# Moving one more slice of a modulation product from VectorE to TensorE, in a prologue that streams its weights from memory

## The chip, the cores and the metric

The kernel runs on one core of one Trainium2 chip. The metric is device time in microseconds, from the start of the program to its end. The engines carry these names: PE is TensorE (matmuls; PEld is its weight loads), DVE is VectorE, ACT is ScalarE, POOL is GpSimd and SP is SyncE, which here only starts transfers. An engine works through its own instructions in order, and engines wait for each other with semaphores that count up.

## What is computed

Two transformer-like blocks in float32, 256 tokens of width 2048. Only the start of the first block matters here. A condition vector c is multiplied with a large matrix, and the result shifts and scales a normed input, which then meets the weights `a_w_in`:

```python
silu_c = jax.nn.silu(c)                              # c: 1 x 2048
m_l = (silu_c @ ada_w[i] + ada_b[i]).reshape(bsz, 1, N_MOD, D_MODEL)   # ada_w: 2048 x 12288
n_l = modulate(rmsnorm(h_lat, norm_g[i, 0]), m_l[:, :, 0], m_l[:, :, 1])   # h * (1 + scale) + shift
z = jax.nn.gelu(h @ w_in)                            # in chunk_mlp_mix, with h = n_l; w_in: 2048 x 8192
```

The shift is the first 2048 columns of the product and the scale the second 2048. Everything else in the first block follows on z, and the second block on the first.

## The kernel before, in words

**The prologue.** Shift and scale are made in four groups g = 0 to 3 of 512 output columns each, and with each group four more tiles of 128 input channels of n_l (k = 4g to 4g+3) become ready. For a group, eight slices d = 0 to 7 of `ada_w` are loaded into `mods`, which has four slots: slice t = 8g + d goes to slot t % 4. A slice is 256 rows of the matrix times 512 columns of the shift and 512 of the scale, and two transfers bring it (L368). SP starts them in order, and before slice t it waits until slice t - 4 has been used.

**Two ways to use a slice.** On DVE (`mod_group`) a slice takes two operations on 128x1024 elements (L1086 for the first of a group, L1089 for the others), which add slice times condition value into `acc`. On PE (`mod_column`, L1790) a slice takes 16 small matmuls, with 128x128 of the slice as the weights and one column of the condition as the moving operand, so that the sum over rows comes out in a few PSUM columns. `PE_MOD` lists the slices of each group that go to PE: 6 in group 0, and 2 in groups 1, 2 and 3. The rest goes to DVE. When DVE has added its last slice, `mod_last` (L1801) sums `acc` over the partitions with eight matmuls of the same small kind. `mod_gain` on DVE (L1098 to L1101) adds the partial sums and writes `acol`, which is the group's gain, and `mcol`, which holds its shift.

**The weight units.** `a_w_in` comes in slabs of 1 MB into `raw` (L348), four slabs deep, and each slab is two units of 128x2x512. For each unit ACT writes a rounded copy `whi` (`cast`, L521), DVE writes the remainder `wlo` (`lo`, L1029), and PE does 12 matmuls of 512 columns (`tok_unit`, L1722). Group g has the six units u = 6g to 6g+5. With a group's gain, ACT and DVE make the four tiles of n_l: DVE writes `n1full` (L1137) for the first two and ACT for the others, ACT writes the rounded `xth` (L627), and DVE writes the remainder `xtl` (L1141). The group's first unit needs the first two `xtl` tiles and the `lo` of unit 6g, and its second unit needs the other two.

**The order on each engine,** for group g:

- PE: `mod_last(g)`, units 6g to 6g+3, `mod_column(g+1, 2)`, units 6g+4 and 6g+5. Group 0 has `mod_column(0, 6)` ahead of all.
- DVE: the adds of the group (with `lo` of the previous group's last two units after slices 0 and 1), `lo` of units 6g and 6g+1, `mod_gain(g)`, `n1full`, `xtl`, `lo` of units 6g+2 and 6g+3.
- ACT: the casts of units 6g and 6g+1, then, with the gain there, the tiles, then the other casts.
- SP: the slices 0 to 7 of the group (each behind its slot), three slabs, and then the next group. Behind group 3 it sends 20 more slabs and 16 transfers for another part of `ada_w`. A slab waits until `lo` of the units that lay in its place is done.

Slice 6 of groups 1 to 3 lies in the slot of slice 2, and so it waits for `mod_column(g, 2)` on PE. Behind the prologue follow the rest of the first block and the whole second block, both with PE at work almost throughout.

Of the kernel before, what the change touches and what calls it, by code (L numbers as in the profile page):

```python
# [24 lines left out]
P = 128  # L25
# [41 lines left out]
QUAD_AT = tuple(12 + 3 * n for n in range(16))  # L67
Q_TURN_AT = (10, 20, 29, 38)
TURN_BANK = (2, 3, 4)
PE_MOD = ((6,), (2,), (2,), (2,))  # L70


def first_unit(u):
# [7 lines left out]
    return sum(2 for i in range(4) for e in range(8) if e not in PE_MOD[i] and (i, e) <= (g, d))  # L81


def mod_columns(g, last=True):

    return 2 * g + 3 + last


HALVES = list(range(16, 32)) + list(range(16))
# [94 lines left out]
def program(nc, a, out):  # L184
    with ExitStack() as ctx:
# [156 lines left out]
        def _(sp):  # L342
# [14 lines left out]
            for g in range(4):  # L357
                for d in range(8):
                    t = 8 * g + d
                    if t >= 4:  # L360
                        g0, d0 = (t - 4) // 8, (t - 4) % 8
                        if d0 in PE_MOD[g0]:
                            sp.wait_ge(mod_turned, mod_columns(g0, False))
                        else:
                            sp.wait_ge(mod_added, mod_adds(g0, d0))
                    src = ada_w[d * 256:d * 256 + 256, 0:2 * D].rearrange("(k p) (j n) -> p k j n", p=P, j=2)
                    for i in range(2):
                        sp.dma_start(mods[:, t % 4, i], src[:, i, :, g * 512:g * 512 + 512]).then_inc(mod_loaded[t % 4], 8 * 2)  # L368
                for c in range(3):
                    s = 3 * g + c  # L370
                    slab(s // 4, s % 4, w_in, g, c * 512 + GW)
            for n in range(20):
                slab(G_IN + 3 + n // 4, n % 4, w_in, n % 4, n // 4 * 512 + (3 * 512 + GW))
                if n % 5 < 4:
                    k = n - n // 5
                    if k >= 4:
                        sp.wait_ge(mod_added, mod_adds(3, 7) + k - 3)
                    elif 4 + k in PE_MOD[3]:
                        sp.wait_ge(mod_turned, mod_columns(3, False))
                    else:  # L380
                        sp.wait_ge(mod_added, mod_adds(3, 4 + k))
                    sp.dma_start(ada2[:, k % 4], ada_w[k * P:k * P + P, 2 * D:3 * D]).then_inc(mod_loaded[k % 4], 16)
# [38 lines left out]
        def _(pool):  # L421
# [37 lines left out]

            pool.wait_ge(sem("ss_n1"), 2)  # L460
            rsqrt("n1", 0, 4, 2, 1.0 / D, EPS1)
            pool.wait_ge(mod_turned, mod_columns(3))
            acc_start(2, acc[:, 0], 0)
            acc_start(3, acc[:, 1], 1)
            stream_ada(3, 0, 0, 2)
# [45 lines left out]
        def _(act):  # L511
# [97 lines left out]
                load(gvb[:, :], a["a_g_v"][0:1, bass.ds(c * 512, 512)].broadcast_to([P, 512]), "gv_loaded")  # L609

            for g in range(4):
                for u in (6 * g, 6 * g + 1):
                    cast(G_IN + u // 8, u % 8, g == 0)
                act.wait_ge(sem("gain_n1"), g + 1)
                for i in range(6):
                    u = 6 * g + i
                    if i > 1:
                        cast(G_IN + u // 8, u % 8, u < 4)
                    for k in (4 * g + 2 * i, 4 * g + 2 * i + 1) if i < 2 else ():
                        if k > 3:  # L620
# [404 lines left out]
        def _(dve):  # L1025
# [68 lines left out]
            def mod_gain(g):  # L1094

                n = len(PE_MOD[g]) + 1
                dve.wait_ge(mod_turned, mod_columns(g))
                own(dve.tensor_reduce(msum[:, :], ps[:, 6 + g % 2, 0:8 * n].rearrange("p (s m) -> p m s", m=8), AX.X, ALU.add))  # L1098
                own(dve.tensor_tensor(mcol[:, 0:2, 4 * g:4 * g + 4], msum[:, :].rearrange("p (j b) -> p j b", b=4),
                                      bcol[:, :, 4 * g:4 * g + 4], ALU.add))  # L1100
                dve.scalar_tensor_tensor(out=acol[:, 4 * g:4 * g + 4], in0=mcol[:, 1, 4 * g:4 * g + 4], scalar=1.0,  # L1101
                                         in1=cols[:, 16 + 4 * g:20 + 4 * g], op0=ALU.add, op1=ALU.mult)\
                   .then_inc(sem("gain_n1"), 1)
# [16 lines left out]
            for g in range(4):  # L1120
                mod_group(g, mod_between(g))
                if g == 0:
# [2 lines left out]
                    own(dve.tensor_copy(fcol[:, :], ps[:, 0, 114:130]))  # L1125
                    own(dve.tensor_copy(cols[:, :], ps[:, 0, 0:114]))
                    dve.tensor_tensor(again[:, :], fcol[:, :], cols[:, C_AN], ALU.mult).then_inc(sem("cols_ready"), 1)
                for u in (6 * g, 6 * g + 1):
                    lo(G_IN + u // 8, u % 8)
                mod_gain(g)  # L1130
                for i in range(4 if g < 3 else 6):
                    u = 6 * g + i
                    if i == 0:
                        dve.wait_ge(sem("gain_n1"), g + 1)
                        dve.wait_ge(sem("start_copied"), 2 * g + 2)
                        for k in (4 * g, 4 * g + 1):
                            own(dve.tensor_scalar(n1full[:, k % 4, :], n1t[:, k, :], acol[:, k:k + 1], mcol[:, 0, k:k + 1],  # L1137
                                                  ALU.mult, ALU.add))
                    for k in (4 * g + 2 * i, 4 * g + 2 * i + 1) if i < 2 else ():
                        dve.wait_ge(sem("nh"), k + 1)  # L1140
                        dve.tensor_tensor(xtl[:, k, :], n1full[:, k % 4, :], xth[:, k, :].bitcast(F32), ALU.subtract)\  # L1141
                           .then_inc(sem("nl"), 1)
                    if i > 1:
                        lo(G_IN + u // 8, u % 8)


# [565 lines left out]
        def _(pe):  # L1712
# [82 lines left out]
            def mod_last(g):  # L1795
# [2 lines left out]
                pe.wait_ge(mod_added, mod_adds(g, 7))  # L1798
                for jb in range(8):
                    c0 = g * 512 + jb % 4 * P  # L1800
                    mm = pe.matmul(ps[:, bank, 8 * s + jb:8 * s + jb + 1], acc[:, jb // 4, c0:c0 + P], ones[:, 0:1],  # L1801
                                   start=True, stop=True)
                mm.then_inc(mod_turned, 1)

            def turned_sums(src):

# [27 lines left out]
            mod_column(0, 6)  # L1834
            for g in range(4):
                mod_last(g)
                if g == 0:
                    pe.wait_ge(sem("start_copied"), 9)
                    pe.wait_ge(sem("cols_ready"), 1)
# [460 lines left out]
```

## Time and profile before

| | us |
|---|---|
| median of 3 runs | 2390.51 |
| lowest and highest | 2387.26 and 2396.4 |
| the profiled execution, whole | 2390.51 |
| its span from first to last instruction | 2388.8 |
| PE busy, share of the span | 96% |
| DVE busy, share of the span | 67% |
| DMA engines busy, in tenths, first six of 40 slices of the span | 9 9 9 9 7 8 |

The profile comes from one execution, and its span is what the engines' records cover. The granted clock (PEclk) of TensorE is 1.00 where it runs at its full 2.4 GHz and 0.50 where it runs at 1.2 GHz. Records of small matmuls in float32 come in pairs, so that a `mod_column` of 16 matmuls shows as 32 records and a `mod_last` of 8 as 16. The prologue covers the first 150 us or so. The mean granted clock of the whole span is 0.983.

### The profile page before, as it was taken

What the parts mean: (1) busy time and instruction counts of PE and PEld (TensorE: products, weight loads), DVE (VectorE), ACT (ScalarE), POOL (GpSimd) and SP (SyncE); (2) the same over time, 40 slices, a digit from 0 to 9 for tenths busy, and PEclk for the clock granted to TensorE, in tenths of its full rate; (3) what the DMA queues carried; (4) which work ended last, traced back from release to release, by engine and by line L of the source; (5) the groups of instructions that cost most, each with busy time, mean ns of one, the idle gap of its engine ahead of it and who ended that gap; (6) DMA issues with size and microseconds to landing.
All of it is one profiled execution on the core that took longest, in us unless ns stands there. A gap on an engine that the chain in (4) does not pass through costs nothing.

```text
span 2388.8 us, 34521 instructions
## 1 busy us (share of the span) xinstructions
PE 2295.3 (96%) x13343; PEld 1996.2 (84%) x13343; DVE 1601.9 (67%) x1973; ACT 1130.2 (47%) x1693; POOL 96.9 (4%) x182
## 2 busy tenths in 40 slices
PE   6789999999989999999999999999999999999897
PEld 5678888887788888888888889999999999778786
DVE  6777677677768865666656776667667646666654
ACT  3345444443365543555445554444444455545443
POOL 0000000111100000000000000000000000000000
PEclk8789999999999999999999999999999999999999
DMA  9999788788857755555555655444444545433352
GB/s 337 357 358 357 255 265 280 232 314 311 317 176 252 271 198 187 183 190 179 194 194 176 210 179 164 157 142 142 142 142 142 167 151 153 146 124 107 106 194 106
DMA packets 229910, 492.95 MB, mean 206 GB/s; under 512 B 9618, under 2 KB 12392, under 8 KB 226696
## 3 DMA queue, kind: packets, MB, share of 16 engines
q1 hardware_dynamic: 210384, 432.05, 53.3%
q0 software_dynamic: 14144, 50.93, 6.4%
q10 hardware_dynamic: 5256, 8.20, 1.0%
q8 instruction: 90, 1.47, 0.3%
q14 instruction: 36, 0.29, 0.0%
HBM read 488.49 MB, written 2.10 MB: 205 GB/s over the span
## 4 chain that ended last, share of the span: by engine, by line
PE 82%; DVE 8%; DMA 4%; issue 2%; ACT 2%; SPq 0%; DVEq 0%; POOL 0%; POOLq 0%; ACTq 0%
PE ps L1722 31%; PE ps L1740 21%; PE ps L1755 14%; PE ps L1757 7%; DMA ada<-in_ada_w 2%; PE ps L2199 2%; DVE wlo L1029 2%; DVE acc L1089 2%; DMA mods<-in_ada_w 1%; PE ps L2026 1%; DMA raw<-in_a_w_in 1%; PE ps L2169 1%; ACT whi L521 1%; DVE acc L1038 1%; PE ps L1866 1%
## 5 line engine op out<-in xcount | busy, mean ns | idle before, releaser
L1029 DVE TENSOR_TENSOR wlo<-raw,whi 128x1024 fp32r<-128x1024 f32 x720 | 872.3, 1222 | 511.1 <-ACT whi L521 509.5
L521 ACT ACTIVATE whi<-raw 128x1024 fp32r<-128x1024 f32 x720 | 755.9, 1057 | 835.2 <-PE ps L1722 406.2
L1755 PE MATMUL ps<-xt__58,whi 128*128 128x512 f32 x1408 | 498.1, 399 | 0.9 <-DVE h L1221 0.7
L1757 PE MATMUL ps<-xt__58,wlo 128*128 128x256 f32 x1408 | 395.3, 281 | 0.0
L1722 PE MATMUL ps<-whi,xt__58 128*128 128x512 f32 x1024 | 331.9, 401 | 11.3 <-DVE xt__58 L1141 11.3
L1740 PE MATMUL ps<-xmh__59,whi 128*128 128x272 f32 x1088 | 323.3, 297 | 3.8 <-DVE ks L1426 3.1
L1755 PEld LDWEIGHTS ps<-xt__58,whi 128*128 128x128 f32 x1408 | 264.5, 188 | 67.3 <-DVE h L1221 2.2
L1740 PE MATMUL ps<-xmh__59,wlo 128*128 128x272 f32 x1088 | 315.7, 290 | 0.0
L1740 PE MATMUL ps<-xml__60,whi 128*128 128x272 f32 x1088 | 313.8, 288 | 0.0
L1757 PEld LDWEIGHTS ps<-xt__58,wlo 128*128 128x128 f32 x1408 | 266.0, 189 | 0.1
L1722 PEld LDWEIGHTS ps<-whi,xt__58 128*128 128x128 f32 x1024 | 196.9, 192 | 53.2 <-DVE xt__58 L1141 8.3
L1740 PEld LDWEIGHTS ps<-xmh__59,whi 128*128 128x128 f32 x1088 | 205.7, 189 | 11.4 <-issue 10.1
L1740 PEld LDWEIGHTS ps<-xml__60,whi 128*128 128x128 f32 x1088 | 205.8, 189 | 0.5
L1740 PEld LDWEIGHTS ps<-xmh__59,wlo 128*128 128x128 f32 x1088 | 205.6, 189 | 0.0
L1722 PE MATMUL ps<-wlo,xt__58 128*128 128x512 f32 x512 | 203.1, 397 | 0.0
L1038 DVE SCALAR_TENSOR_TENSOR acc<-ada,ccol,acc 128x1024 f32<-128x1024 f32 x96 | 122.9, 1280 | 33.9 <-DMA ada<-in_ada_w 33.7
L1722 PE MATMUL ps<-whi,hth 128*128 128x512 f32 x352 | 138.8, 394 | 0.4 <-DVE htl L1302 0.4
L1722 PE MATMUL ps<-whi,htl 128*128 128x512 f32 x352 | 137.2, 390 | 0.0
L1722 PE MATMUL ps<-wlo,hth 128*128 128x512 f32 x352 | 137.0, 389 | 0.0
L1722 PEld LDWEIGHTS ps<-wlo,xt__58 128*128 128x128 f32 x512 | 98.8, 193 | 20.3 <-issue 0.2
L1722 PE MATMUL ps<-whi,ush 128*128 128x512 f32 x256 | 100.5, 392 | 4.2 <-DVE wlo L1029 4.2
L1722 PE MATMUL ps<-wlo,ush 128*128 128x512 f32 x256 | 99.7, 389 | 0.0
(297 smaller groups left out, 3272.6 us busy)
## 6 DMA issues: line engine op xcount, KB each, us to landing
raw<-in_a_w_in SPq DMA_DIRECT2D x128, 1024.0 KB, 5.3
raw<-in_ffn_w_up SPq DMA_DIRECT2D x88, 1024.0 KB, 5.1
ada<-in_ada_w POOLq DMA_DIRECT2D x96, 512.0 KB, 4.6
raw<-in_a_w_out SPq DMA_DIRECT2D x48, 1024.0 KB, 5.3
raw<-in_ffn_w_down SPq DMA_DIRECT2D x44, 1024.0 KB, 5.2
mods<-in_ada_w SPq DMA_DIRECT2D x64, 512.0 KB, 8.8
raw<-in_b_w_in SPq DMA_DIRECT2D x32, 1024.0 KB, 5.4
ada<-in_ada_w SPq DMA_DIRECT2D x16, 1024.0 KB, 12.2
```

The costliest lines, as they stand in the source:

```text
L521: act.activation(whi[:, r % 4], raw[:, r // 2, r % 2], ACT.Copy).then_inc(hi_ready, 1)
L1029: dve.tensor_tensor(wlo[:, r % 4], raw[:, r // 2, r % 2], whi[:, r % 4].bitcast(F32), ALU.subtract).then_inc(lo_ready, 1)
L1038: dve.scalar_tensor_tensor(out=y, in0=ada[:, half], scalar=ccol[:, bass.ds(kt, 1)], in1=y, op0=ALU.mult, op1=ALU.add).then_inc(ada_step, 1)
L1089: dve.scalar_tensor_tensor(out=y, in0=mods[:, d % 4, i], scalar=ccol[:, k:k + 1], in1=y, op0=ALU.mult, op1=ALU.add).then_inc(mod_added, 1)
L1722: mm = pe.matmul(ps[:, bank + tok, :], xs[x], w[:, r % 4, i, :], start=first and i == 0 and n == 0, stop=last and i == 1 and n == 2)
L1740: mm = pe.matmul(ps[:, bank + c, 0:n_tok], ws[w], x[:, 2 * r + i, 0:n_tok], start=first and i == 0 and n == 0, stop=last and i == 1 and n ...
L1755: pe.matmul(both, whi[:, r % 4, i, c * P:c * P + P], xt_[:, :, k * T:k * T + T], start=first and i == 0, stop=last and i == 1, skip_group_ ...
L1757: mm = pe.matmul(ps[:, bank + c, 0:T], wlo[:, r % 4, i, c * P:c * P + P], xth[:, k, :], start=False, stop=last and i == 1, skip_group_chec ...
L1866: mm = pe.matmul(ps[:, 4 + tok, g * 256:g * 256 + 256], wsc[:, tok, g, :], v[:, bass.ds(c, 1), tok, g * 256:g * 256 + 256].rearrange("p o ...
L2026: mm = pe.matmul(ps[:, 7, 0:256], wt[0:w, kb, :], (vx1[(j - back + 1) % 2] if i > 2 else vx0)[0:w, kb, :], start=kb == blocks[0], stop=kb ...
L2169: mm = pe.matmul(ps[e * BH:e * BH + BH, 3, 0:256], vb[0:w, kb, j * BH:j * BH + BH], wtb[0:w, kb, e:4:2, :], start=kb == 0, stop=kb == 1 + tok,
L2199: mm = pe.matmul(y, ws[w], token_cols(x, (2 * r + i) * L), start=r + c % 2 + i + n == 0, stop=r == 7 and i == 1 and n == 2, skip_group_che ...
```

## The change

Slice 7 of each group, the last to arrive, goes to PE. So DVE has six slices to add in a group instead of seven, and PE has two `mod_column` instead of one. The new `mod_column(g, 7)` stands behind `mod_last(g)` in PE's order, and `mod_gain(g)` now waits for it and sums three partial results instead of two. `mod_columns` counts the finished `mod_column` calls, and `mod_last` no longer counts up a semaphore of its own, since the call behind it does. SP now waits for `mod_column(g, 7)` where it waited for slice 7's adds. Also, the `lo` of units 6g and 6g+1 moves on DVE from before `mod_gain` to behind it: `lo` of 6g follows `n1full`, and `lo` of 6g+1 follows the third and fourth `xtl` tile. On ACT the cast of unit 6g stays before the wait for the gain, and that of unit 6g+1 comes behind the first two `xth` tiles.

```diff
@@ -67,7 +67,7 @@
 QUAD_AT = tuple(12 + 3 * n for n in range(16))
 Q_TURN_AT = (10, 20, 29, 38)
 TURN_BANK = (2, 3, 4)
-PE_MOD = ((6,), (2,), (2,), (2,))
+PE_MOD = ((6, 7), (2, 7), (2, 7), (2, 7))
 
 
 def first_unit(u):
@@ -81,9 +81,9 @@
     return sum(2 for i in range(4) for e in range(8) if e not in PE_MOD[i] and (i, e) <= (g, d))
 
 
-def mod_columns(g, last=True):
-
-    return 2 * g + 3 + last
+def mod_columns(g, d):
+
+    return 2 + sum(1 for i in range(4) for e in PE_MOD[i] if (i, e) <= (g, d))
 
 
 HALVES = list(range(16, 32)) + list(range(16))
@@ -360,7 +360,7 @@
                     if t >= 4:
                         g0, d0 = (t - 4) // 8, (t - 4) % 8
                         if d0 in PE_MOD[g0]:
-                            sp.wait_ge(mod_turned, mod_columns(g0, False))
+                            sp.wait_ge(mod_turned, mod_columns(g0, d0))
                         else:
                             sp.wait_ge(mod_added, mod_adds(g0, d0))
                     src = ada_w[d * 256:d * 256 + 256, 0:2 * D].rearrange("(k p) (j n) -> p k j n", p=P, j=2)
@@ -376,7 +376,7 @@
                     if k >= 4:
                         sp.wait_ge(mod_added, mod_adds(3, 7) + k - 3)
                     elif 4 + k in PE_MOD[3]:
-                        sp.wait_ge(mod_turned, mod_columns(3, False))
+                        sp.wait_ge(mod_turned, mod_columns(3, 4 + k))
                     else:
                         sp.wait_ge(mod_added, mod_adds(3, 4 + k))
                     sp.dma_start(ada2[:, k % 4], ada_w[k * P:k * P + P, 2 * D:3 * D]).then_inc(mod_loaded[k % 4], 16)
@@ -459,7 +459,7 @@
 
             pool.wait_ge(sem("ss_n1"), 2)
             rsqrt("n1", 0, 4, 2, 1.0 / D, EPS1)
-            pool.wait_ge(mod_turned, mod_columns(3))
+            pool.wait_ge(mod_turned, mod_columns(3, 7))
             acc_start(2, acc[:, 0], 0)
             acc_start(3, acc[:, 1], 1)
             stream_ada(3, 0, 0, 2)
@@ -609,12 +609,11 @@
                 load(gvb[:, :], a["a_g_v"][0:1, bass.ds(c * 512, 512)].broadcast_to([P, 512]), "gv_loaded")
 
             for g in range(4):
-                for u in (6 * g, 6 * g + 1):
-                    cast(G_IN + u // 8, u % 8, g == 0)
+                cast(G_IN + 6 * g // 8, 6 * g % 8, g == 0)
                 act.wait_ge(sem("gain_n1"), g + 1)
                 for i in range(6):
                     u = 6 * g + i
-                    if i > 1:
+                    if i:
                         cast(G_IN + u // 8, u % 8, u < 4)
                     for k in (4 * g + 2 * i, 4 * g + 2 * i + 1) if i < 2 else ():
                         if k > 3:
@@ -1094,7 +1093,7 @@
             def mod_gain(g):
 
                 n = len(PE_MOD[g]) + 1
-                dve.wait_ge(mod_turned, mod_columns(g))
+                dve.wait_ge(mod_turned, mod_columns(g, 7))
                 own(dve.tensor_reduce(msum[:, :], ps[:, 6 + g % 2, 0:8 * n].rearrange("p (s m) -> p m s", m=8), AX.X, ALU.add))
                 own(dve.tensor_tensor(mcol[:, 0:2, 4 * g:4 * g + 4], msum[:, :].rearrange("p (j b) -> p j b", b=4),
                                       bcol[:, :, 4 * g:4 * g + 4], ALU.add))
@@ -1125,8 +1124,6 @@
                     own(dve.tensor_copy(fcol[:, :], ps[:, 0, 114:130]))
                     own(dve.tensor_copy(cols[:, :], ps[:, 0, 0:114]))
                     dve.tensor_tensor(again[:, :], fcol[:, :], cols[:, C_AN], ALU.mult).then_inc(sem("cols_ready"), 1)
-                for u in (6 * g, 6 * g + 1):
-                    lo(G_IN + u // 8, u % 8)
                 mod_gain(g)
                 for i in range(4 if g < 3 else 6):
                     u = 6 * g + i
@@ -1136,11 +1133,12 @@
                         for k in (4 * g, 4 * g + 1):
                             own(dve.tensor_scalar(n1full[:, k % 4, :], n1t[:, k, :], acol[:, k:k + 1], mcol[:, 0, k:k + 1],
                                                   ALU.mult, ALU.add))
+                        lo(G_IN + u // 8, u % 8)
                     for k in (4 * g + 2 * i, 4 * g + 2 * i + 1) if i < 2 else ():
                         dve.wait_ge(sem("nh"), k + 1)
                         dve.tensor_tensor(xtl[:, k, :], n1full[:, k % 4, :], xth[:, k, :].bitcast(F32), ALU.subtract)\
                            .then_inc(sem("nl"), 1)
-                    if i > 1:
+                    if i:
                         lo(G_IN + u // 8, u % 8)
 
 
@@ -1798,9 +1796,8 @@
                 pe.wait_ge(mod_added, mod_adds(g, 7))
                 for jb in range(8):
                     c0 = g * 512 + jb % 4 * P
-                    mm = pe.matmul(ps[:, bank, 8 * s + jb:8 * s + jb + 1], acc[:, jb // 4, c0:c0 + P], ones[:, 0:1],
+                    pe.matmul(ps[:, bank, 8 * s + jb:8 * s + jb + 1], acc[:, jb // 4, c0:c0 + P], ones[:, 0:1],
                                    start=True, stop=True)
-                mm.then_inc(mod_turned, 1)
 
             def turned_sums(src):
 
@@ -1834,6 +1831,7 @@
             mod_column(0, 6)
             for g in range(4):
                 mod_last(g)
+                mod_column(g, 7)
                 if g == 0:
                     pe.wait_ge(sem("start_copied"), 9)
                     pe.wait_ge(sem("cols_ready"), 1)
```

## Rows read from the trace of the kernel before

**Rows 1.** The profile page: span, and DMA issues (count, KB each, us to landing).

```profile
span 2388.8 us, 34521 instructions
...
mods<-in_ada_w SPq DMA_DIRECT2D x64, 512.0 KB, 8.8
```

**Rows 2.** Windows (columns: length, busy by engine, PEclk, DMA share, GB/s), group 2.

```profile
90.00:92.00 2.00, 2.00 (x19) 2.00 (x20) 1.86 (x2) 0.00 (x0) 0.00 (x0) 1.00 0.07 26
```

**Rows 3.** The chain of waits (start, us, what), in the prologue and behind it.

```profile
59.30 7.30 DMA mods<-in_ada_w
...
144.00 127.28 PE ps L1722 x552
```

**Rows 4.** The timeline of PE from group 1 to group 3 (start, us, idle before).

```profile
54.21 3.63 PE L1790 MATMUL ps<-ccol,mods 128*128 128x1 f32 x32
...
69.28 3.57 PE L1801 MATMUL ps<-ones,acc 128*128 128x1 f32 x16 [5.84 <-DVE acc L1089]
75.21 0.79 PE L1722 MATMUL ps<-whi,xt__58 128*128 128x512 f32 x1 [2.35 <-DVE xt__58 L1141]
...
88.37 3.63 PE L1790 MATMUL ps<-ccol,mods 128*128 128x1 f32 x32
...
122.63 3.51 PE L1790 MATMUL ps<-ccol,mods 128*128 128x1 f32 x31
```

**Rows 5.** The timeline of DVE in group 1.

```profile
52.24 8.01 DVE L1089 SCALAR_TENSOR_TENSOR acc<-mods,ccol,acc 128x1024 f32<-128x1024 f32 x6
...
63.87 2.60 DVE L1089 SCALAR_TENSOR_TENSOR acc<-mods,ccol,acc 128x1024 f32<-128x1024 f32 x2 [3.61 <-DMA mods<-in_ada_w]
66.63 2.60 DVE L1089 SCALAR_TENSOR_TENSOR acc<-mods,ccol,acc 128x1024 f32<-128x1024 f32 x2
...
70.41 2.36 DVE L1029 TENSOR_TENSOR wlo<-raw,whi 128x1024 fp32r<-128x1024 f32 x2 [1.19 <-ACT whi L521]
72.89 0.17 DVE L1098 TENSOR_REDUCE msum<-ps 128x8 f32<-128x16 f32 x1
...
73.30 0.16 DVE L1101 SCALAR_TENSOR_TENSOR acol<-mcol,cols 128x4 f32<-128x4 f32 x1
73.50 0.86 DVE L1137 TENSOR_SCALAR n1full<-n1t,acol,mcol 128x256 f32<-128x256 f32 x2
74.40 0.76 DVE L1141 TENSOR_TENSOR xt__58<-n1full,xt__58 128x256 fp32r<-128x256 f32 x2
...
77.54 2.36 DVE L1029 TENSOR_TENSOR wlo<-raw,whi 128x1024 fp32r<-128x1024 f32 x2 [0.52 <-ACT whi L521]
```

**Rows 6.** The timeline of DVE and PE in group 0.

```profile
18.25 10.72 DVE L1089 SCALAR_TENSOR_TENSOR acc<-mods,ccol,acc 128x1024 f32<-128x1024 f32 x8
...
28.91 4.23 PE L1790 MATMUL ps<-ccol,mods 128*128 128x1 f32 x32 [1.38 <-DMA mods<-in_ada_w]
31.61 2.60 DVE L1089 SCALAR_TENSOR_TENSOR acc<-mods,ccol,acc 128x1024 f32<-128x1024 f32 x2 [2.63 <-DMA mods<-in_ada_w]
...
34.27 3.57 PE L1801 MATMUL ps<-ones,acc 128*128 128x1 f32 x16 [1.12 <-DVE acc L1089]
...
38.96 0.16 DVE L1101 SCALAR_TENSOR_TENSOR acol<-mcol,cols 128x4 f32<-128x4 f32 x1
...
41.07 0.77 PE L1722 MATMUL ps<-whi,xt__58 128*128 128x512 f32 x1 [3.23 <-DVE xt__58 L1141]
```

**Rows 7.** Windows of 1 us around the granted clock's fall in group 0.

```profile
30.00:31.00 1.00, 1.00 (x11) 1.00 (x10) 0.00 (x0) 0.00 (x0) 0.00 (x0) 1.00 1.06 389
...
32.00:33.00 1.00, 1.00 (x6) 1.00 (x6) 0.96 (x2) 0.00 (x0) 0.00 (x0) 0.50 1.11 399
```

**Rows 8.** The same windows around `mod_last` and the units of group 1.

```profile
70.00:71.00 1.00, 1.00 (x6) 1.00 (x6) 0.59 (x1) 1.00 (x2) 0.00 (x0) 0.50 1.04 383
...
80.00:81.00 1.00, 1.00 (x6) 0.83 (x5) 0.96 (x2) 0.57 (x1) 0.00 (x0) 1.00 1.06 391
```

**Rows 9.** The timeline of SP behind the last group.

```profile
140.91 0.37 SPq L348 DMA_DIRECT2D raw<-in_a_w_in  x1
```

## The prediction

> **What bounds the kernel now.** I read the page first: PE is busy 96% of a span of 2388.8 us [rows 1], so whatever is won must be won where PE waits, and what delays PE is likely to reach the end. The windows of 20 us then showed that PE's waits lie in the first 150 us, and the chain of waits showed that behind them PE works without a gap: one piece of 127.28 us of units starts at 144.00 [rows 3]. So the question is when group 3's first unit starts on PE. Before the change that is at 144.00.
>
> I then read the prologue's timelines. The groups repeat with a period of 34.2 us: `mod_column(1, 2)` ends at 54.21 + 3.63 = 57.84 and `mod_column(2, 2)` at 88.37 + 3.63 = 92.00 [rows 4]. I call this end Y, since it frees the slot that slice 6 waits for. A group moves 16 transfers of 512 KB and three slabs of 1 MB, together 11.5 MB, and at the 389 GB/s of a full window [rows 7] that takes 29.7 us. So the transfers alone don't set the 34.2 us. The window of 90 to 92 us shows DMA at a share of 0.07 [rows 2]: the queue is empty, because SP holds slice 6 back until Y. The loop goes like this, in group 1:
>
> - At Y = 57.84 slice 6 is let go. Its adds start at 63.87, that is Y + 6.03, and they end 2.60 later at Y + 8.63 [rows 5].
> - Slice 7 is there by 66.63, and its adds end at 69.23 [rows 5]. `mod_last` runs from 69.28 to 72.85 [rows 4].
> - The gain is ready 0.61 later, at 73.30 + 0.16 = 73.46 [rows 5].
> - `n1full` and two `xtl` follow, and PE starts the first unit at 75.21 [rows 4], that is Y + 17.37.
> - Four units and the next `mod_column` take from 75.21 to 92.00, which is 16.79, and 17.37 + 16.79 = 34.2.
>
> Every part of that loop is on the path, also where DVE is the one at work.
>
> **What the change takes from the path.** The two adds of slice 7, with the wait for the slice: `mod_last` now starts when slice 6 is added, at Y + 8.66 instead of Y + 11.44 (69.28). That is 2.78 us a group. DVE has 2.60 us less to do, and this is all that it gives.
>
> **What it adds: `mod_column(g, 7)`.** It stands behind `mod_last`, and the gain waits for it. It has 32 records. At the full clock the same 32 take 3.63 [rows 4]. But what clock will it get? `mod_last` in group 1 has 16 records in 3.57, 0.223 us each, under a granted clock of 0.50, the lower level of 1.2 GHz [rows 4, 8], while the full-clock ones take 3.63 / 32 = 0.113 each. At the lower level 32 records cost 32 x 0.223 = 7.14. The clock had been at 0.50 since shortly before, because PE had sat idle for 5.84 [rows 4]; now it idles some 3 us there. Group 0 shows that the small matmuls don't bring the clock up or even hold it: PE is busy without a gap with `mod_column(0, 6)` from 28.91, at 1.00 in the window from 30, and at 0.50 in the window from 32, still in the same block [rows 6, 7]. In the window from 80 it is 1.00 again, after some 5 us of 512-column units [rows 8, 4]. So I take 7.14 for each of the four, after a `mod_last` of 3.57. The bounds from both sides are the all-warm pair, 1.81 + 3.63 = 5.44, and the all-cold pair, 3.57 + 7.14 = 10.71.
>
> On this the Trainium skill ("TensorE: Matmul & The Clock Gate", section "LDWEIGHTS (loading the stationary operand)") says that loading weights costs a time that goes by their 128 columns over 1.2 a nanosecond, and names no dependence on the gate. By it 32 loads of 107 ns would cost 3.4 us at either level, and the sum below would be smaller by about 3.7 in each of the four groups. The row of `mod_last` speaks against that, since its time per record doubles at 0.50.
>
> **What it moves on DVE and ACT.** `lo` of units 6g and 6g+1 lay between `mod_last`'s start and the gain, 70.41 to 72.77 [rows 5], and cost nothing: PE's sums covered them. Now the first follows `n1full` and stands ahead of the first two `xtl`, 1.18 us (half of 2.36), on the path to PE's first unit. With `n1full` and the two `xtl` (73.46 to 75.16, 1.70) the first unit starts 2.93 behind the gain instead of 1.75; I add 1.15. The cast of 6g+1 is also moved behind the gain, about 1 us on ACT. The second unit then needs, behind the gain, two `xth`, this cast, two tiles of two operations each, and on DVE two `xtl` and a `lo`, together some 5.8 us. PE is in its first unit until gain + 2.9 + 5 (at 0.50), so that is covered, and by a hair even at the full clock (2.9 + 2.7). The `lo` of the third and fourth unit end about gain + 8.1, before PE asks for them.
>
> Is DVE late anywhere next? It starts the next group's slices at gain + 8.1 instead of gain + 6.4 (77.54 + 2.36 - 73.46), and needs 15 us for slices 0, 1 and 3 to 5 with two `lo` (those of group 2 start at 79.90, which is 45.7 a period earlier, and group 1's end at 60.25 [rows 5]). It is done at gain + 23. Slice 6 lands at gain + 2.9 + 16.8 + 6.0 = gain + 25.7. So 2.6 us of slack are left and the cost is nothing.
>
> **SP.** Slice 3 of the next group now waits for `mod_column(g, 7)`, at about Y + 19.4, where it waited for slice 7's adds at Y + 11.4. The transfers ahead of it (slices 6 and 7, three slabs, the next group's 0, 1 and 2, at 2.7 us per MB) keep the queue full until Y + 25, and so it costs nothing. Behind the last group, a slab that waits for `lo` of unit 19 starts at 140.91 now [rows 9], 3.1 before PE's first unit, and will start 2.9 behind it. The queue may then run empty for some 5 us. The unit that needs this slab is the ninth from there, 22 us on, and I cost it at nothing; without that cover it would be up to 6.
>
> **The sum.**
>
> - Group 0. The adds of slices up to 5 end at 28.97, slice 7 is there by 31.61 [rows 6], and `mod_column(0, 6)` ends at 33.14. Then `mod_last` and the new block follow: 33.14 + 3.57 + 7.14 = 43.85, the gain comes at 44.5 instead of 39.12, and the first unit at 47.4 instead of 41.07 [rows 6]: **+6.3**. From there to Y, four units and a `mod_column`, I take the same time as before.
> - Groups 1 and 2. From Y to the first unit: 8.66 + 3.57 + 7.14 + 0.61 + 2.93 = 22.9 instead of 17.37: **+5.5** each.
> - Group 3 has 144.00 - (122.63 + 3.51) = 17.86 before [rows 3, 4] and 22.9 after: **+5.0**.
>
> Together +22.3. The clock may still be at 1.00 for part of a `mod_last`, since PE's idle time ahead of it is shorter by 2.8; for that I take off about half a microsecond in three groups, and reach +21. The profiled execution took 2390.51, 1.7 more than its span, and is itself the median of the runs: 2390.5 + 21 = **2411.5 us**, slower by 0.9%.
>
> **The rivals.** Changes of under 0.5% (12 us) can't be told from none here.
>
> - *The full clock holds through the new block.* The skill's rule for it ("TensorE: Matmul & The Clock Gate", "Part 1: The HAM clock gate") is that sustained PE activity takes the clock to 2.4 GHz; by that rule 8 us of unbroken matmuls might count as activity, whatever their width. Worked out from rows: the pair costs 5.44, so from Y to the first unit it takes 8.66 + 5.44 + 0.61 + 2.93 = 17.6 (+0.3), and the units, at 1.00 from their start, save some 2.4 (in group 1 they run at 0.50 from 75.21 to about 80 [rows 4, 8], and half of that is lost). Each of the four groups then wins 2 to 2.5, and the total is about -9: 2381.5 us. This is the rival that ends on the other side: it decides if the blocks get 1.00. Group 0's fall in the middle of such a block [rows 7] speaks against it. 7 in 100.
> - *The clock is at 1.00 for part of each block*, for one of the two in most groups. Each `mod_last` at the full clock saves 1.8, and each new block 3.5. With half of all that, 10 us come off: 2401, which is inside the 0.5%. 12 in 100.
> - *The transfers absorb it.* If the loads were the bound, later PE work would cost nothing and the time would stay at 2390. The share of 1.04 to 1.06 in the full windows [rows 7, 8] speaks for it, and the empty queue at 90 us [rows 2] against. 5 in 100.
> - *The late slab or the shuffled `lo` also costs.* PE stalls for the second or third unit in each group, or for slabs behind the last: another 6 to 10, 2419. 12 in 100.
> - The forecast itself, 2405 to 2416: 64 in 100.
>
> So slower by over 0.5%: 0.64 + 0.12 and a third of the second rival, 0.80. Faster: only part of the first, 0.04. The same: 0.16. The range of 2396 to 2420 leaves out the first and third rival and little else.
>
> **What would show it.** In the profile after: PE's new L1790 block right behind L1801 in each group, about 7 us long under a clock of 0.50; the ends of `mod_column(g, 2)` near 64, 104 and 143, a period of 39.7; the first unit of group 3 near 165; no new PE waits behind it; DMA windows emptier than before. I am wrong if that block is 3.6 long, or if the first unit of group 3 is at 165 and the end is not.

## The result and the profile after

The changed kernel takes 2409.03 us in the median of six runs (2406.97 to 2411.72), the kernel before 2393.84 in the six beside it (2387.26 to 2396.72). The ratio is 1.0063, with a 95% interval from 1.0051 to 1.0076: 0.63% slower, about 15 us. The profiled execution took 2411.31, with a span of 2409.6.

PE's timeline of the changed kernel, in the order of time (start, us, idle before). L1788 is `mod_column`, L1799 `mod_last` and L1720 a unit; they answer to [rows 4, 6].

```profile
28.19 4.38 PE L1788 MATMUL ps<-ccol,mods 128*128 128x1 f32 x32 [1.47 <-DMA mods<-in_ada_w]
32.44 3.55 PE L1799 MATMUL ps<-ones,acc 128*128 128x1 f32 x16
35.85 6.96 PE L1788 MATMUL ps<-ccol,mods 128*128 128x1 f32 x32
46.52 0.77 PE L1720 MATMUL ps<-whi,xt__58 128*128 128x512 f32 x1 [3.70 <-DVE xt__58 L1139]
...
59.89 3.63 PE L1788 MATMUL ps<-ccol,mods 128*128 128x1 f32 x32
...
71.48 3.09 PE L1799 MATMUL ps<-ones,acc 128*128 128x1 f32 x16 [2.36 <-DVE acc L1088]
74.44 6.96 PE L1788 MATMUL ps<-ccol,mods 128*128 128x1 f32 x32
84.90 0.80 PE L1720 MATMUL ps<-whi,xt__58 128*128 128x512 f32 x1 [3.50 <-DVE xt__58 L1139]
...
99.84 1.70 PE L1788 MATMUL ps<-ccol,mods 128*128 128x1 f32 x14
109.59 1.95 PE L1799 MATMUL ps<-ones,acc 128*128 128x1 f32 x16 [0.81 <-DVE acc L1088]
111.40 5.52 PE L1788 MATMUL ps<-ccol,mods 128*128 128x1 f32 x32
120.42 0.80 PE L1720 MATMUL ps<-whi,xt__58 128*128 128x512 f32 x1 [3.50 <-DVE xt__58 L1139]
134.33 4.48 PE L1788 MATMUL ps<-ccol,mods 128*128 128x1 f32 x32
146.72 1.95 PE L1799 MATMUL ps<-ones,acc 128*128 128x1 f32 x16
148.52 5.13 PE L1788 MATMUL ps<-ccol,mods 128*128 128x1 f32 x32
158.10 0.80 PE L1720 MATMUL ps<-whi,xt__58 128*128 128x512 f32 x1 [4.45 <-DVE xt__58 L1139]
```

Each L1799 now has a second L1788 right behind it: the new block, 6.96, 6.96, 5.52 and 5.13 us for the same 32 records. Y, where `mod_column(g, 2)` ends, comes at 63.52, 101.54 and 138.81; the row at 99.84 shows only the last 14 of that call's 32 records, which begins at 97.92. Group 3's first unit starts at 158.10 instead of 144.00 [rows 3].

DVE's timeline of the changed kernel in group 1, as in [rows 5]:

```profile
68.82 2.61 DVE L1088 SCALAR_TENSOR_TENSOR acc<-mods,ccol,acc 128x1024 f32<-128x1024 f32 x2 [2.78 <-DMA mods<-in_ada_w]
81.44 0.18 DVE L1097 TENSOR_REDUCE msum<-ps 128x8 f32<-128x24 f32 x1 [10.01 <-PE ps L1788]
...
81.86 0.16 DVE L1100 SCALAR_TENSOR_TENSOR acol<-mcol,cols 128x4 f32<-128x4 f32 x1
82.06 0.86 DVE L1134 TENSOR_SCALAR n1full<-n1t,acol,mcol 128x256 f32<-128x256 f32 x2
82.95 1.23 DVE L1028 TENSOR_TENSOR wlo<-raw,whi 128x1024 fp32r<-128x1024 f32 x1
84.09 0.75 DVE L1139 TENSOR_TENSOR xt__58<-n1full,xt__58 128x256 fp32r<-128x256 f32 x2
```

DVE has slice 6 added at 71.43 and then stands idle for 10.01 us until PE is done. The work that it was spared has turned into waiting. Behind the gain (82.02), the `lo` at 82.95 stands between `n1full` and the `xtl` that PE's first unit needs.

Windows of 1 us of the changed kernel, in the new block of group 2 (columns as in [rows 2]; the third number from the end is the granted clock):

```profile
112.00:113.00 1.00, 1.00 (x11) 1.00 (x11) 0.00 (x0) 0.00 (x0) 0.00 (x0) 1.00 1.06 412
113.00:114.00 1.00, 1.00 (x6) 1.00 (x7) 0.00 (x0) 0.68 (x1) 0.00 (x0) 0.50 1.04 403
```

PE is busy in both without a gap, and the clock falls from 2.4 to 1.2 GHz between them: 11 records in one, 6 in the next. This is [rows 7] again, in another group.

### The profile page after: what moved, and what is told of

It is laid out like the page before. It is cut to its first block, busy times and chain, and to the rows that moved or that the text cites. A ratio compares the mean times of both kernels' runs of the same rounds, so it can differ in the third digit from the quotient of the medians.

```text
span 2409.6 us, 34765 instructions
## 1 busy us (share of the span) xinstructions
PE 2325.0 (96%) x13471; PEld 2022.9 (84%) x13471; DVE 1591.6 (66%) x1965; ACT 1130.4 (47%) x1693; POOL 97.5 (4%) x182
## 4 chain that ended last, share of the span: by engine, by line
PE 84%; DVE 7%; DMA 4%; issue 2%; ACT 2%; POOL 0%; SPq 0%; DVEq 0%; POOLq 0%; ACTq 0%
PE ps L1720 33%; PE ps L1738 20%; PE ps L1753 13%; PE ps L1755 6%; DMA ada<-in_ada_w 3%; PE ps L2197 2%; PE ps L1788 2%; DVE wlo L1028 2%; DMA mods<-in_ada_w 1%; PE ps L2024 1%; PE ps L2167 1%; DVE acc L1037 1%; PE ps L1864 1%; ACT eb__132 L938 1%; PE ps L2043 1%
## 5 line engine op out<-in xcount | busy, mean ns | idle before, releaser
L1720 PE MATMUL ps<-whi,xt__58 128*128 128x512 f32 x1024 | 334.8, 404 | 15.2 <-DVE xt__58 L1139 15.2
L1720 PEld LDWEIGHTS ps<-whi,xt__58 128*128 128x128 f32 x1024 | 199.2, 195 | 57.8 <-DVE xt__58 L1139 11.7
L1720 PE MATMUL ps<-wlo,xt__58 128*128 128x512 f32 x512 | 205.0, 400 | 0.0
L1720 PE MATMUL ps<-whi,hth 128*128 128x512 f32 x352 | 138.8, 394 | 0.4 <-DVE htl L1300 0.4
L1720 PE MATMUL ps<-whi,htl 128*128 128x512 f32 x352 | 137.2, 390 | 0.0
L1720 PE MATMUL ps<-wlo,hth 128*128 128x512 f32 x352 | 137.0, 389 | 0.0
L1720 PEld LDWEIGHTS ps<-wlo,xt__58 128*128 128x128 f32 x512 | 99.7, 195 | 20.8 <-issue 0.2
L1720 PE MATMUL ps<-whi,ush 128*128 128x512 f32 x256 | 101.2, 395 | 4.6 <-DVE wlo L1028 4.6
L1720 PE MATMUL ps<-wlo,ush 128*128 128x512 f32 x256 | 100.2, 391 | 0.0
```

Of the source, the lines that this page charges most:

```text
L1720: mm = pe.matmul(ps[:, bank + tok, :], xs[x], w[:, r % 4, i, :], start=first and i == 0 and n == 0, stop=last and i == 1 and n == 2)
```

## The experiments

Each kernel was timed in five rounds against the kernel before. For reading the profiles I use two marks of one execution: the start of group 3's first unit, and the start of the four spreading matmuls that close PE's first long stretch of units (shown as `x8` behind `x552` in the chain of waits). The second mark is the better one, because it also holds what the clock does in the first units. Chain of waits of the kernel before, then of the changed one (start, us, what):

```profile
271.28 3.43 PE ps L1814 x8
...
462.99 19.06 PE ps L1722 x84
...
868.79 3.43 PE ps L1814 x8
872.22 70.75 PE ps L1722 x312
...
2288.22 87.33 PE ps L1722 x384
```

```profile
158.10 128.28 PE ps L1720 x552
286.38 3.43 PE ps L1811 x8
...
478.09 19.06 PE ps L1720 x84
...
886.60 3.43 PE ps L1811 x8
890.03 70.75 PE ps L1720 x312
...
2308.99 87.34 PE ps L1720 x384
```

The shift is 14.1 at the first mark, 15.1 at the second, and still 15.1 at 478.09. Up to 886.60 it grows by 2.7 and up to 2308.99 by another 3.0, in code that the change doesn't touch. This is no part of the change: over ten of the profiles (the two kernels and the first eight experiments) the stretch from the piece of 84 records (478.09) to the next `x8` (886.60) takes anything from 404.3 to 412.6, and that from the piece of 312 to the last of 384 from 1416.0 to 1419.5, with no order by kernel. So two profiled spans (20.8 apart here) can't be subtracted, and the second mark's 15.1 agrees with the 15.2 between the medians.

| kernel | 1st mark | 2nd mark | against before | ratio, interval |
|---|---|---|---|---|
| before | 144.00 | 271.28 | | |
| changed | 158.10 | 286.38 | +15.1 | 1.0063, 1.0051 to 1.0076 |
| e1 block only | 151.57 | 279.84 | +8.6 | 1.0032, 1.0020 to 1.0044 |
| e2 order only | 149.20 | 277.40 | +6.1 | 1.0022, 1.0012 to 1.0032 |
| e3 short block | 140.26 | 267.19 | -4.1 | 0.9986, 0.9977 to 0.9995 |
| e4 early column | 137.43 | 265.30 | -6.0 | 0.9975, 0.9964 to 0.9986 |
| e5 changed, kept busy | 159.75 | 285.17 | +13.9 | 1.0061, 1.0039 to 1.0082 |
| e6 before, kept busy | 143.45 | 270.29 | -1.0 | 1.0013, 1.0001 to 1.0025 |
| e7 early, kept busy | 134.96 | 261.87 | -9.4 | 0.9971, 0.9959 to 0.9984 |
| e8 slice 6 | 143.75 | 270.53 | -0.8 | 1.0009, 0.9998 to 1.0021 |
| e9 slice 6, early | 139.22 | 266.03 | -5.3 | 0.9978, 0.9966 to 0.9991 |
| e10 slice 6, two early | 141.33 | 268.32 | -3.0 | 0.9978, 0.9966 to 0.9990 |
| e11 early, order, busy | 134.98 | 263.07 | -8.2 | 0.9964, 0.9950 to 0.9978 |

The fourth column is the second mark's, in us; 0.1% of the ratio is 2.4 us. A mark comes from one profiled execution. For e6, e7, e8 and e10 it differs from what the ratio says by 2.3 to 4.1 us, so a difference of that size between two kernels is not shown by their marks.

### e1 and e2: the two halves of the change

e1 is the changed kernel with the old order on ACT and DVE. e2 is the kernel before with the new order only, and `PE_MOD` as it was. The lines marked with a minus are those that e1 puts back, and those with a plus are what e2 adds:

```diff
-                for u in (6 * g, 6 * g + 1):
-                    lo(G_IN + u // 8, u % 8)
                 mod_gain(g)
...
+                        lo(G_IN + u // 8, u % 8)
...
-                    if i > 1:
+                    if i:
                         lo(G_IN + u // 8, u % 8)
```

> The changed kernel with the casts and lo of units 6g and 6g+1 back where they were before the change, so that only slice 7's move to PE is left. My theory (each piece from slice 6's release to the next is on one loop): the first unit comes 1.15 us sooner behind the gain in each of four groups, so this is about 4.6 us faster than the changed kernel and about 10.5 us slower than the kernel before. Rival A (the moved lo are covered by something else and cost nothing): as slow as the changed kernel, 15 us above before. Rival B (the moved lo are the whole loss, the block on PE being hidden): within 3 us of before.

> The kernel before with only the casts and lo of units 6g and 6g+1 moved behind the gain, slice 7 still on DVE. My theory: 4 x 1.15 = 4.6 us slower than before, with the first unit 2.9 us behind the gain in groups 0 to 2. Rival A (covered): the same as before within 1 us. Rival B (the moved lo are the whole loss): 15 us slower.

Both halves cost. The block alone is 0.32% slower, 7.6 us, where I had expected 10.5; the order alone is 0.22%, 5.3 us, where I had expected 4.6. Rival B for either is out, and so is rival A. Together they make 12.9 by the ratios and 14.7 by the marks, beside 15.1 for both at once: the halves add up within what the intervals allow. PE's first units in e2:

```profile
77.08 0.79 PE L1720 MATMUL ps<-whi,xt__58 128*128 128x512 f32 x1 [3.50 <-DVE xt__58 L1139]
...
111.93 0.79 PE L1720 MATMUL ps<-whi,xt__58 128*128 128x512 f32 x1 [3.49 <-DVE xt__58 L1139]
```

PE waits 3.50 for `xtl` behind `mod_last`, where it waited 2.35 [rows 4]. That is the 1.15 of the sum, to the digit.

### e3: the block made short

```diff
-                for jb in range(8):
+                for jb in range(1 if d == 7 else 8):
```

with the partial sum of slice 7 kept out of `mod_gain`.

> The changed kernel, but mod_column of slice 7 does one of its eight column blocks (4 records instead of 32), and its result isn't summed into the gain: slice 7's share of the modulation is left out. The semaphores and the order are those of the change. My theory: a group keeps the 2.8 us won by the adds that went, loses 1.15 by the moved lo and 0.5 to 0.9 by the short block; together 0.7 to 1.1 us won per group, 3 to 4 us faster than before and 18 to 19 faster than the changed kernel. Rival (the cost is the wait or the changed order of release for slice 3, not the block's length): still 10 us or more above before.

0.14% faster than before, 3.4 us, and 4.1 by the mark, as my theory has it. All semaphores, the release of slice 3's slot by PE, and the new order are in it. What is gone is 28 of 32 records per group. So the loss of the block is its length on PE, not the wait that came with it. That the adds taken off DVE are worth their 2.6 us a group fits this: Y to the first unit of group 1 takes 16.37 here, 1.00 less than before, although the moved `lo` (1.15) and the short block (0.99) are in it. (Its `mod_last` is 1.3 shorter, and slice 6's adds come 1.1 later, which nearly cancel.) But no run measures the adds by themselves.

### e4: slice 6 let go one unit earlier

```diff
-                    if u == 6 * g + 3 and g < 3:
+                    if u == 6 * g + 2 and g < 3:
                         mod_column(g + 1, 2)
```

> The kernel before with mod_column(g+1, 2) on PE one unit earlier, behind the third unit of a group instead of the fourth. My theory (slice 6 waits for the end of this call, and the whole group for slice 6): 2.7 us less in each of groups 1 to 3, 8 us faster than before in all, a period of 31.5 instead of 34.2. Rival A (the loads or DVE's adds bound the group): the same as before within 2 us, and DVE without idle time ahead of slice 6's adds.

0.25% faster, 6 us by ratio and by mark; I had expected 8. The loop is as I read it. DVE in groups 1 to 3 of e4:

```profile
61.08 2.61 DVE L1089 SCALAR_TENSOR_TENSOR acc<-mods,ccol,acc 128x1024 f32<-128x1024 f32 x2 [0.63 <-DMA mods<-in_ada_w]
...
65.50 2.61 DVE L1089 SCALAR_TENSOR_TENSOR acc<-mods,ccol,acc 128x1024 f32<-128x1024 f32 x2 [1.82 <-DMA mods<-in_ada_w]
...
85.47 10.73 DVE L1089 SCALAR_TENSOR_TENSOR acc<-mods,ccol,acc 128x1024 f32<-128x1024 f32 x8
96.55 2.61 DVE L1089 SCALAR_TENSOR_TENSOR acc<-mods,ccol,acc 128x1024 f32<-128x1024 f32 x2 [0.36 <-DMA mods<-in_ada_w]
...
116.25 13.44 DVE L1089 SCALAR_TENSOR_TENSOR acc<-mods,ccol,acc 128x1024 f32<-128x1024 f32 x10
```

DVE's idle time ahead of slice 6's adds is down from 3.61 [rows 5] to 0.63 in group 1, and in the other two groups they follow on slice 5's without a gap. Group 1 now waits 1.82 for slice 7, which ends last there. The chain of waits of e4 shows what ends last in group 2:

```profile
89.73 9.45 DMA raw<-in_a_w_in
...
100.29 2.36 DVE wlo L1029 x2
102.66 0.09 DVE msum L1098
```

It is the group's first weight slab, and behind it the cast and the two `lo` that stand ahead of the gain. Group 3 has the same chain, from a slab at 120.87 on. `mod_last` is over by then (99.21 + 1.95 = 101.16 in group 2). The slab stands behind slice 6 in SP's order, so its chain still begins at the end of `mod_column`, but it no longer goes through DVE's adds: with the early column slice 7 ends last in group 1, and the slab in groups 2 and 3. The groups win 1.0, 3.6 and 1.9 where 2.7 each were expected; in group 3 `n1full` also takes 2.89 for two tiles, where it took 1.75.

### e5, e6 and e7: matmuls that nobody reads, to hold the clock

```diff
+            def busy(g, n):
+                for _ in range(n if g else 0):
+                    pe.matmul(ps[:, 6 + (g + 1) % 2, 32:512], xt_[:, 0, 0:P], xt_[:, 0, 0:480], start=True, stop=True)
...
+                busy(g, 22)      # e5: 14, e7: 14
                 mod_last(g)      # e5: and mod_column(g, 7)
+                busy(g, 5)       # e5: 7
```

> The changed kernel with extra matmuls of 480 columns on PE that nobody reads, in the gaps of groups 1 to 3 in which PE is idle: 14 ahead of mod_last and 7 behind the new block, ahead of the first unit. They cost PE only idle time, if they fit. My theory (PE's low clock is part of the new block's price and of the units' start): mod_last runs at 1.00, the block partly, and the units start warm; 5 to 8 us faster than the changed kernel, 7 to 10 slower than before. Rival (the clock plays no part, the records cost what they cost): the same as the changed kernel or slower by what the extra matmuls add.

> The kernel before with the same extra matmuls, 22 ahead of mod_last in groups 1 to 3 and 5 behind it. My theory: mod_last costs 1.8 instead of 3.6 and the units save up to 2.4, so 3 to 4 us less in each of three groups, 8 to 12 us faster than before. Rival (the small matmuls lower the clock in any case before the units start, or the extra ones are late): only mod_last gains, 3 to 5 us faster or the same.

> The kernel before with mod_column(g+1, 2) one unit earlier and the extra matmuls (14 and 5). If both act on the same loop, their gains add until the loads bound a group at 29.7 us: 11 to 15 us faster than before. Rival (the early column has already left DVE or the loads as the bound): no better than the early column alone, 5 to 6 us faster than before.

These are the lines of e6; the comments give the counts of the other two, and where e5 differs. e5 gave nothing (1.0061 beside the changed kernel's 1.0063), and that doesn't speak for the rival. PE's timeline of e5 in groups 1 and 3:

```profile
69.10 3.19 PE L1805 MATMUL ps<-xt__58 128*128 128x480 f32 x14
72.14 1.84 PE L1799 MATMUL ps<-ones,acc 128*128 128x1 f32 x16
73.84 4.07 PE L1788 MATMUL ps<-ccol,mods 128*128 128x1 f32 x32
...
142.52 3.19 PE L1805 MATMUL ps<-xt__58 128*128 128x480 f32 x14
146.70 1.95 PE L1799 MATMUL ps<-ones,acc 128*128 128x1 f32 x16 [0.98 <-DVE acc L1088]
148.50 6.79 PE L1788 MATMUL ps<-ccol,mods 128*128 128x1 f32 x32
```

Two things went wrong. Slice 6 was added at 67.53 + 2.61 = 70.14, but the extra matmuls ran until 72.14, so they held `mod_last` up by 2 us, and in group 2 by 2.5. And where they ended early enough, in group 3, the block of 32 records still took 6.79, although the wide matmuls had ended only 2.8 us ahead of it, and `mod_last`, which lay between behind 0.98 of idle time, ran at 1.00. In groups 1 and 2 the block took 4.07 and 4.73, where the changed kernel has 6.96 and 5.52. So the extra matmuls may help a block or not, and three blocks don't show which it will be. e5 was badly built, and leaves the price of the clock to the rows.

e6 was expected 8 to 12 us faster and came out 0.13% slower, an interval that almost reaches 1; by the mark it is 1.0 faster. `mod_last` did drop to 1.84 to 1.95. But look at DVE in group 1 of the kernel before [rows 5]: `lo` of unit 6g+1 ends at 72.77 and the gain's first step starts at 72.89. PE's `mod_last` ended at 72.85, so two chains ended within 0.1 us of each other, and the profile names only one. With `mod_last` shortened by 1.6, the `lo`, and through ACT's cast the first slab, hold the gain where it was: its first step starts at 72.75 in group 1 of e6. The chain of waits of e6 in group 3 shows that:

```profile
126.95 8.80 DMA raw<-in_a_w_in
...
135.78 1.07 ACT whi L521
...
136.87 2.36 DVE wlo L1029 x2
139.23 0.10 DVE msum L1098
```

That is a term that I hadn't seen: the units' data and `mod_last` are a tie in the kernel before, and in e4 the units' data are the later of the two. It also says what the moved `lo` are good for. They cost 1.15 as long as `mod_last` or a block is the later of the two, and can gain only when it isn't; e11 tries that. The 0.13% by which e6 is slower is not explained by its marks, and its cause stays open.

e7 has both the early column and the extras: 0.29% faster than before, 6.9 us (9.4 by the mark), where 11 to 15 were expected. It is a little ahead of e4, but the intervals overlap, so the rival (no better than the early column alone) isn't excluded.

### e8, e9 and e10: slice 6 instead of slice 7

```diff
-PE_MOD = ((6,), (2,), (2,), (2,))
+PE_MOD = ((6,), (2, 6), (2, 6), (2, 6))
...
+                if g:
+                    mod_column(g, 6)
                 mod_last(g)
```

In e9 `mod_column(g+1, 2)` stands one unit earlier, and in e10 two.

> The kernel before with slice 6 instead of slice 7 given to PE in groups 1 to 3, as mod_column(g, 6) ahead of mod_last; the lo and casts as before. The block then runs while slice 7 lands and while DVE adds it. My theory: DVE's last adds end where they did, the block ends between there and 1.7 us later, and so the time is 0 to 5 us above before, against 7.6 for slice 7's move alone. Rival (a second block of 32 records costs the same wherever it stands in PE's order): as slow as slice 7's move alone, 7 to 8 us or more above before.

> The kernel with slice 6 on PE and its block ahead of mod_last, and mod_column(g+1, 2) one unit earlier. My theory: PE's own work is the bound of a group then (six units, two blocks of 3.6, mod_last 3.6 and the gap behind the gain, 31 to 32 us), so DVE's relief gives nothing on top of the early column: 5 to 7 us faster than before. Rival (with the early column DVE is the bound, its idle time ahead of slice 6's adds having shrunk to 0.4 to 0.6 us, and a slice less on DVE pays): 9 us or more faster than before.

> The same with mod_column(g+1, 2) two units earlier, behind the group's second unit. My theory: the same bound by PE's work, 31 to 32 us a group, so the same as with one unit earlier within 2 us. Rival (DVE's relief makes room for slice 6's earlier release): 2.7 us less in each of three groups, 12 us or more faster than before.

e8 is 1.0009 (0.9998 to 1.0021): the same number of slices on PE as the change in groups 1 to 3, and no loss that can be told from none. PE's timeline of e8 shows why:

```profile
64.19 3.63 PE L1790 MATMUL ps<-ccol,mods 128*128 128x1 f32 x32
69.09 3.57 PE L1801 MATMUL ps<-ones,acc 128*128 128x1 f32 x16 [1.27 <-DVE acc L1089]
```

The block of slice 6 runs at the full clock, straight behind the units, while slice 7 lands. It ends at 67.8, before DVE's adds at 69.0, and `mod_last` even waits 1.27 for DVE. So in this profile the block is off the path, and so it is in groups 2 and 3, where `mod_last` waits 0.74 and 1.09 for DVE. There is no gain either: DVE's two adds of slice 7 are back on the path. But e8 leaves group 0 as it was, so it must be held against e1 without group 0. Group 0's first unit starts at 45.87 in e1 and at 41.07 before [rows 6], and group 3's at 151.57 and 144.00 [rows 3]: of e1's 7.6 us, 4.8 are group 0's and only 2.8 the other three's. Those 2.8 are all that the better place could save. By the mark e8 has them (-0.8 against before), but by the ratio it is 2.2 us slower than before, with an interval that goes up to 5, so the timings don't show that the place of the block in groups 1 to 3 matters. In e1 a group's way from Y to the first unit is 0.6, 0.0 and 1.1 longer than before: there the block, 5.5 us long, is nearly paid for by the adds that went and by a `mod_last` that takes 1.8 instead of 3.6. Group 0 is the dearest, since it already had slice 6's block in the same place: PE does two blocks and `mod_last` in a row there, most of it at 0.50, while DVE, done with its adds at 28.2, could have had slice 7 ready by 34.2 [rows 6].

e9 and e10 are both 0.9978. As expected, freeing DVE adds nothing to the early column, and two units earlier gains nothing over one. In e9 DVE has slice 7 added at 98.62 in group 2, but PE is still in its block, and `mod_last` starts only at 100.35; in groups 1 and 3 the two end within 0.4 of each other. So with slice 6 on PE, it is PE's own work that ends last in group 2, and the relief of DVE is spent.

### e11: early column, the new order, and fewer extras

> The kernel before with the early column, with lo and casts of units 6g and 6g+1 behind the gain, and with 7 extra matmuls of 480 columns ahead of mod_last and 5 behind it. Where mod_last takes 1.8, the gain was seen to wait for lo of unit 6g+1 and so for the first slab; moved behind the gain these lo no longer hold it back. My theory: the gain comes 1.5 to 2 us sooner per group than with the early column and extras alone, the first unit 0.5 us sooner, and DVE's later start takes the rest: 9 to 12 us faster than before, 1 to 4 faster than early column and extras. Rival (DVE or the loads are the bound by then): no better than early column and extras, 6 to 8 us faster than before, or worse by the 1.15 us per group of the moved lo.

It is the fastest kernel of the study by ratio, 0.36% under the kernel before (8.6 us), just under the 9 to 12 that were expected. Beside e7 (0.29%) the intervals overlap, and its second mark is 1.2 later than e7's, so nothing says that it is faster than e7, and the rival isn't excluded. DVE in group 2 of e11:

```profile
83.81 13.44 DVE L1088 SCALAR_TENSOR_TENSOR acc<-mods,ccol,acc 128x1024 f32<-128x1024 f32 x10 [0.56 <-DMA mods<-in_ada_w]
99.29 0.17 DVE L1097 TENSOR_REDUCE msum<-ps 128x8 f32<-128x16 f32 x1 [2.04 <-PE ps L1799]
```

The gain comes 2.04 behind DVE's last add, which is `mod_last` at the full clock and nothing else, and DVE works from slice 3 to slice 7 in one piece. The 1.15 of the moved `lo` is still there: in group 1 the first unit starts 2.89 behind the gain, and 1.74 in e7. But the gain comes 2.6 behind DVE's last add and not 4.5 as in e7, and so here the moved `lo` don't show as a loss.

## Why the prediction was right, step by step

- **The loop.** Confirmed by e4 (slice 6 let go earlier, 6 us won where 8 were expected) and by e3.
- **The adds that go.** `mod_last` starts at once when slice 6 is added (71.48, 109.59, 146.72). What they are worth is seen only together with the other terms, in e3.
- **The new block.** I took 7.14 for each, and they took 6.96, 6.96, 5.52 and 5.13, with `mod_last` at 3.4, 3.0, 1.8 and 1.8 instead of 3.57. The clock was at 0.50 for the whole of it in groups 0 and 1, and fell in the midst of the block in groups 2 and 3. So the forecast and the second rival (the full clock for part) each hold for half of the groups. This is the largest term that was mis-sized: pair by pair, `mod_last` and block took 10.4, 9.9, 7.3 and 6.9 instead of 10.7, 8 us less in all. With it, 22.9 from Y to the first unit in each group became 21.4, 18.9 and 19.3. The first rival, the full clock throughout, is out: in none of the four blocks did it hold. The Trainium skill's figure for weight loads ("TensorE: Matmul & The Clock Gate", section "LDWEIGHTS (loading the stationary operand)"), which names no dependence on the gate, doesn't fit the trace: 32 records take 6.96 at 0.50 and 3.63 at 1.00.
- **The moved `lo`.** 1.15 per group expected, 1.15 seen in e2's waits. The first unit starts 2.88 behind the gain in groups 1 and 2 (2.93 forecast). In group 3 it is 3.83, because `n1full` takes 1.81 there for two tiles; the kernel before has 1.75 in the same place.
- **From Y to slice 6's adds** I took group 1's 6.03. The changed kernel has 5.30, 5.40 and 5.25, and groups 2 and 3 of the kernel before, whose adds start at 97.57 and 131.40, had 5.57 and 5.14 behind Y. (Group 3's Y is 122.63 + 3.63 = 126.26. The row of 3.51 in [rows 4] has 31 of the 32 records, so the 17.86 of the sum should be 17.74.) One group out of three was no good choice for a term that counts three times.
- **What was costed at nothing.** There is no new wait of PE behind the prologue, though DMA does run empty near 160, as forecast. But the way from the first unit to the next Y, taken as unchanged, is so only in groups 0 and 1 (+0.2 and -0.1). In group 2 it takes 18.39 instead of 16.69: the units stay at 0.50 until 126, and the clock falls again inside `mod_column(3, 2)`, which takes 4.48 instead of 3.63. These 1.7 us the prediction didn't have.
- **The sum.** At group 3's first unit the terms come to +5.45 for group 0 (6.3 forecast), +4.01, +1.30 and +1.55 from Y to the first unit in groups 1 to 3 (5.5, 5.5 and 5.0 forecast), and +1.79 between the first units and Y (nothing forecast), together 14.1 for a forecast of 22.3. So most of the miss is in groups 2 and 3, where the clock was better than assumed. For the whole kernel +21 was forecast; it is +15.1 by the mark and 15.2 by the medians. The absolute time, 2411.5 against 2409.03, looks closer than the difference was, because the later runs of the kernel before have a median 3.3 above the one that I started from. That closeness is luck. The direction and the path were right by their reasons; the size was some 40% too large. The rival of the late slab or shuffled `lo` is not seen.

Left open: what the clock alone costs the changed kernel. e5 was to measure it and didn't. By the rows, four blocks at 3.63 instead of what they took would be 10 us less; this is an estimate for the blocks alone, and it assumes that nothing else ends later.

## What to carry to other kernels

Before work is moved to relieve an engine, look at where the receiving engine would do it. Behind the last sum everybody waits for it, and in group 0, in which PE already was the later engine, that cost 4.8 us (e1). In the other groups the same block cost less than 3 us in all there, and no more than can be told from none behind the units, while a transfer landed (e8). When the profile names one releaser for a wait, look for a second that ends within a few tenths, since it takes over as soon as the first is shortened (e6). And find what lets the next transfer go: here one unit's difference in the place of one call was worth 6 us (e4), and taking a slice off DVE as well added nothing (e9).

## What the runs showed of the hardware

- Blocks of matmuls with one moving column let PE's granted clock fall from 1.00 to 0.50 while PE is busy without a gap: in group 2 of the changed kernel at 113 us, and in group 3 of e5 at 149 us, 3 us behind wide matmuls and 2 behind an idle time of 0.98 (6.79 for 32 records). They don't always do so: in e8 three such blocks, straight behind the units, took 3.62 or 3.63. The Trainium skill ("TensorE: Matmul & The Clock Gate", "Part 1: The HAM clock gate") describes the gate as following how busy PE is; in the window of 113 us the profile shows PE at 100% and the clock falls all the same.
- Whether it falls in a given block differs between groups of one execution: 32 records took 6.96 and 5.13 in the same program, and 3.63, 4.07, 4.38 and 4.73 elsewhere (the changed kernel and e5). In code that no kernel changed, the stretches between marks differ by up to 8 us from one profiled execution to another, which is more than half of the effect that was to be measured.
